# Delta-rule heads: the attention matrices move from VectorE to GpSimd, and the gate sums' fetch to an earlier wait

## What is computed

```python
gc = jnp.cumsum(g, axis=-1)
decay = jnp.exp(jnp.where(incl, gc[..., :, None] - gc[..., None, :], -jnp.inf))
lhs = eye + jnp.einsum("nbhik,nbhjk->nbhij", kb, k) * decay * (1.0 - eye)
u = solve(lhs, v * beta[..., None])
w = solve(lhs, kb * jnp.exp(gc)[..., None])
attn = jnp.einsum("nbhik,nbhjk->nbhij", q, k) * decay
...
def step(state, inp):
    v_new = u_c - jnp.einsum("bhck,bhkv->bhcv", w_c, state)
    o = jnp.einsum("bhck,bhkv->bhcv", q_c, state) + jnp.einsum("bhij,bhjv->bhiv", attn_c, v_new)
    state = state * gl[..., None, None] + jnp.einsum("bhck,bhcv->bhkv", k_c, v_new)
```

## Time and profile before

| | |
|---|---|
| median of 3 runs | 1743.07 us (1726.6 to 1747.39) |
| profiled execution | 1737.7 us |
| its span, first to last instruction | 1735.9 us |
| mean granted clock of TensorE over the span | 0.975 |
| busy: PE, DVE, ACT, POOL | 93%, 50%, 36%, 7% |

### The profile page before, as it was taken

How to read it: one execution, slowest core, us unless ns; L and a number is a source line. 1 busy time by engine, 2 the same in 40 slices (tenths; PEclk the granted TensorE clock), 3 DMA queues, 4 the chain that set the end, 5 groups by cost and what they waited for, 6 DMA issues and landing times.

```text
span 1735.9 us, 35476 instructions
## 1 busy us (share of the span) xinstructions
PE 1610.5 (93%) x14468; PEld 963.2 (55%) x14468; DVE 860.5 (50%) x1952; ACT 620.9 (36%) x1276; POOL 115.8 (7%) x278
## 2 busy tenths in 40 slices
PE   5999999999999999999999999999999888777798
PEld 2465564654755566666575766676744544333343
DVE  1372451722624567786868686868610641111163
ACT  2151531513412446464646464645400112111123
POOL 6000010000000000000000000000000022112100
PEclk9999999969999999999999999999999989999999
DMA  9230110301201212121111111111064589999741
GB/s 358 93 101 2 49 50 0 98 0 49 98 13 56 85 41 73 36 64 51 49 51 49 51 49 51 49 51 49 2 217 173 206 308 419 421 420 409 310 156 49
DMA packets 105458, 210.80 MB, mean 121 GB/s; under 512 B 10323, under 2 KB 78136, under 8 KB 92029
## 3 DMA queue, kind: packets, MB, share of 16 engines
q1 hardware_dynamic: 99256, 197.46, 31.5%
q0 software_dynamic: 4896, 8.40, 1.3%
q10 hardware_dynamic: 1188, 3.28, 0.5%
HBM read 203.73 MB, written 14.81 MB: 126 GB/s over the span
## 4 chain that ended last, share of the span: by engine, by line
PE 54%; DMA 11%; DVE 2%; ACT 2%; issue 1%; SPq 0%; DVEq 0%; POOL 0%; ACTq 0%; POOLq 0%
PE ps L1474 12%; DMA W<-in_moe_w_up_dram 10%; PE ps L1485 6%; PE ps L2497 5%; PE ps L1615 4%; PE ps L1641 4%; PE ps L3079 3%; PE ps L2893 3%; PE ps L515 2%; PE ps L1515 2%; PE ps L1495 1%; PE ps L1525 1%; PE ps L1499 1%; PE ps L1537 1%; PE ps L2906 1%; PE ps L2398 1%
## 5 line engine op out<-in xcount | busy, mean ns | idle before, releaser
L1474 PE MATMUL ps<-hT,W 128*128 128x512 f32 x512 | 231.5, 597 | 2.3 <-ACTq L95 2.2
L1474 PEld LDWEIGHTS ps<-hT,W 128*128 128x128 f32 x512 | 95.4, 191 | 99.9 <-issue 97.8
L603 PE MATMUL ps<-hT,W 128*128 128x512 f32 x288 | 145.4, 635 | 4.2 <-DVE spare L194 4.2
L1485 PE MATMUL ps<-hT,W 128*128 128x512 f32 x256 | 124.5, 615 | 0.0
L2035 DVE SCALAR_TENSOR_TENSOR arena<-ps,arena 128x510 f32<-128x510 f32 (+1 forms) x128 | 95.4, 745 | 14.1 <-ACT arena L1770 10.7
L2497 PE MATMUL ps<-W,yT 128*128 128x512 f32 x216 | 93.1, 592 | 1.3 <-DVE yT L2151 1.3
L603 PEld LDWEIGHTS ps<-hT,W 128*128 128x128 f32 x288 | 52.1, 197 | 52.8 <-issue 51.0
L1615 PEld LDWEIGHTS ps<-W,arena 64*64 64x64 f32 x2048 | 63.4, 135 | 27.9 <-issue 27.9
L2893 PE MATMUL ps<-W,yT 128*32 128x256 f32 x1024 | 58.1, 380 | 20.2 <-DMA W<-in_moe_w_gate_dram 11.8
L1615 PE MATMUL ps<-W,arena 64*64 64x32 f32 x2048 | 67.5, 220 | 6.4 <-ACT arena L1838 3.8
L2970 ACT ACTIVATE arena<-arena 128x256 f32<-128x256 f32 x48 | 20.0, 417 | 147.9 <-DVE arena L2607 136.6
(11 more groups left out here) (533 smaller groups left out, 2818.1 us busy)
## 6 DMA issues: line engine op xcount, KB each, us to landing
W<-in_w_in_dram SPq DMA_DIRECT2D x33, 512.0 KB, 6.7
W<-in_gdn_w_in_dram SPq DMA_DIRECT2D x16, 1024.0 KB, 7.0
arena<-in_moe_w_up_dram SPq DMA_DIRECT2D x16, 1024.0 KB, 6.0
arena<-in_moe_w_down_dram SPq DMA_DIRECT2D x16, 1024.0 KB, 10.0
W<-in_moe_w_up_dram SPq DMA_DIRECT2D x16, 1024.0 KB, 6.0
W<-in_moe_w_down_dram SPq DMA_DIRECT2D x16, 1024.0 KB, 5.8
W<-in_moe_w_gate_dram SPq DMA_DIRECT2D x16, 1024.0 KB, 5.7
arena<-in_moe_w_gate_dram SPq DMA_DIRECT2D x14, 1024.0 KB
```

The source lines that it names most:

```text
L603: mm = pe.matmul(ps[:, 5 + i % 2, :], w[:, k, j, :], hT[:, k, :], start=(k == 0), stop=(k == ND - 1))
L1474: mm = pe.matmul(ps[:, 6 + k0 % 2, :], wg[:, k, j * P:(j + 1) * P], hT[:, k, :], start=(k == 0), stop=(k == ND - 1))
L1485: mm = pe.matmul(ps[:, (4, 1)[e], :], wz[:, k, e * P:(e + 1) * P], hT[:, k, :], start=(k == 0), stop=(k == ND - 1))
```

## The change

`attention` goes from VectorE's list to GpSimd's, which gets a semaphore of its own in each stage (`s.pool`). GpSimd makes the matrices of chunks 0, 3, 1 and 2 in one go, behind "qk masked", "D c" and, in a turn, behind "o 3", the last reading of the old ones. TensorE's wait for "attention 2" moves from the scan's step 1 to step 0. VectorE's `masked_qk` waits for the matrices of the turn before, since it overwrites `qkm`. SyncE waits for "attention 2" of the turn before instead of this one ahead of the gate sums.

```diff
@@ sync: the loop over turns
-            sp.wait_ge(*loop.dve.at("attention 2", i))
+            sp.wait_ge(*loop.pool.at("attention 2", i - 1))
             gate_sums_in(i + 1)
             sp.wait_ge(*loop.pe.at("projected", i))
...
@@ tensor: attended(s, st)
-            if st == 1:
-                pe.wait_ge(*s.dve.at("attention 2", s.i))
+            if st == 0:
+                pe.wait_ge(*s.ago.pool.at("attention 2", s.ago.i))
...
@@ gpsimd
+        def attention(s, c):
+
+            pool.wait_ge(*s.act.at(f"D {c}", s.i))
+            for d in range(2):
+                pool.tensor_tensor(attnT[:, c, 2 * d:2 * d + 2, :], XD[:, 2 * d:2 * d + 2, c * P:c * P + P],
+                                   repeat(qkm[:, c, d, :], 2), ALU.mult).then_inc(*s.pool.step(f"attention {c}"))
+
+        s = first
+        pool.wait_ge(*s.dve.at("qk masked"))
+        for c in (0, 3, 1, 2):
+            attention(s, c)
+        s.pool.close()
+        pool.wait_ge(*s.pool.end())
+        loop.pool.credit(pool)
+        for i in range(LOOPS):
+            s = turn_of(i)
+            s.pool.begin(i)
+            pool.wait_ge(*s.pe.at(f"o {NT - 1}", s.i))
+            pool.wait_ge(*s.dve.at("qk masked", s.i))
+            for c in (0, 3, 1, 2):
+                attention(s, c)
+            s.pool.close()
...
@@ vector: masked_qk(s)
             dve.wait_ge(*s.pe.at("k q", s.i))
+            if s.ago:
+                dve.wait_ge(*s.ago.pool.at("attention 2", s.ago.i))
...
@@ vector: levels(s, scan)
             scan_columns(s, scan)
-            attention(s, 0, s)
             for lv in range(1, LEVELS):
...
-                if lv == 2:
-                    attention(s, NT - 1, s)
...
@@ vector: a turn (and the last stage in the same way)
             decayed_v(s, 0)
-            for c in (1, 2):
-                attention(s, c, s.ago)
             state(s, 0)
```

More of the change, by code:

```diff
@@ L1345, in build, with __init__ @@
     class Stage:
[L1350 to L1356, removed]
+        def __init__(self, pe, dve, act, pool, i=None, ago=None):
+            self.pe, self.dve, self.act, self.pool, self.i, self.ago = pe, dve, act, pool, i, ago
+    first = Stage(steps("first_head_products"), steps("first_head_vector"), steps("first_head_scalar"), steps("first_head_attention"))
+    loop = Stage(steps("heads_products"), steps("heads_vector"), steps("heads_scalar"), steps("heads_attention"))
+    last = Stage(steps("last_head_products"), steps("last_head_vector"), steps("last_head_scalar"), None,
+                 ago=Stage(loop.pe, loop.dve, loop.act, loop.pool, LOOPS - 1))
     def turn_of(i):
-        return Stage(loop.pe, loop.dve, loop.act, i, Stage(loop.pe, loop.dve, loop.act, i - 1))
+        return Stage(loop.pe, loop.dve, loop.act, loop.pool, i, Stage(loop.pe, loop.dve, loop.act, loop.pool, i - 1))
     def next_head(s, each):
@@ L1436, in _ @@
         gr_in.begin(LOOPS - 1)
-        sp.wait_ge(*loop.dve.at("attention 2", LOOPS - 1))
+        sp.wait_ge(*loop.pool.at("attention 2", LOOPS - 2))
         gate_sums_in(LOOPS)
@@ L2151, in gated_y @@
                 dve.tensor_tensor(yT[:, k, :], ps[:, 3 + e, :], zg[:, e, :], ALU.mult).then_inc(*s.dve.step(f"{kind}y {e}"))
[L2153 to L2159, removed]
         def changed(g, lv):
@@ L2311, in _ @@
         s.dve.close()
-    GDN = [(s, None) for s in (ab_pe, ab_dve, ab_act, ab_pool, first.pe, first.dve, first.act)]\
-        + [(s, LOOPS) for s in (loop.pe, loop.dve, loop.act)] + [(s, None) for s in (last.pe, last.dve, last.act)]
+    GDN = [(s, None) for s in (ab_pe, ab_dve, ab_act, ab_pool, first.pe, first.dve, first.act, first.pool)]\
+        + [(s, LOOPS) for s in (loop.pe, loop.dve, loop.act, loop.pool)] + [(s, None) for s in (last.pe, last.dve, last.act)]
     cut[0] = 0
```

## The result

| | before | after |
|---|---|---|
| median, us | 1743.51 (4 runs, 1726.6 to 1747.39) | 1789.63 (4 runs, 1778.83 to 1794.57) |
| profiled execution, us | 1737.7 | 1793.24 |
| its span, us | 1735.9 | 1791.5 |
| mean granted TensorE clock | 0.975 | 0.954 |

The ratio is 1.0275, 95% interval 1.0191 to 1.036: slower beyond the noise; whether by more than 2% the interval leaves open. The median lies 18.6 us above the forecast of 1771 and 0.6 us above the upper end of its range.

A forecast was written before the change was run, and what follows sets the result against it. The prediction took TensorE to bound the heads, with one VectorE piece on its path. The profiled 1737.7 us plus 21 for the hold and 12 for the clock gave 1771 us, with a range of 1740 to 1789.

The forecast's parts named there:

- What bounds the heads: Delta-rule heads, 600 to 1250 us: TensorE bounds, busy 636.76 of 650 us; one VectorE piece before level 1 on its path.
- The removal worth 0: Taking 64 multiplications, 23.1 us, off VectorE gains 0, since nobody waits for them; bounds 0 and 9 us.
- The gate sums, some 7 us sooner and worth 0: SyncE's gate-sum transfer, queued behind the z weights, goes out some 7 us sooner, not half a turn; worth 0.
- The hold on VectorE: Before level 1, GpSimd's SBUF reads block VectorE instructions with two SBUF inputs: 3.0 us a turn, 21 us over seven.
- Copies held, the count by turns: Predicated copies and GpSimd instructions alternate, one each, at 0.56 us a hold: 3.0 us a turn.
- The sign to look for, 3.2: If right, the first group's four predicated copies take some 3.2 us instead of 1.47.
- The first rival: Predicated copies before level 1 are not held: 3 us of delay, pauses of about 1.1 us, 1741 us; chance 0.16.
- the third: GpSimd starts only after the first levels, beside the convolution: price 0 to -3 us, 1736 us; chance 0.10.
- The clock: TensorE's longer pause before level 1 lowers its clock in half the turns: 3.5 x 3.4 = 12 us; bounds 0 and 24.
- the second rival: The clock falls behind the pause in every turn: 1737.7 + 21 + 24 = 1783 us, upper bound 1793; chance 0.25.
- The first head worth 0: In the first head GpSimd's eight multiplications lie beside the convolution, which reads PSUM, so the hold costs 0.
- The range: 1740 to 1789 us, taking in the first rival and most of the second, leaving out the third.

The follow-up runs named there:

- The spread order: Second z half's eighths reordered, one filling the pause before level 1: against before, 0.9959 with VectorE's multiplications; 0.9955 with them on GpSimd, started behind the second first-level transpose.
- the VectorE delay: Before, with three extra unread VectorE multiplications of 128x400 ahead of the first group's predicated copies in each turn: 1793.02 us, ratio 1.0299.
- the late gate sums: The changed kernel, with SyncE's gate-sum fetch also waiting for the first step's decayed values on VectorE: 1801.47 us, ratio 1.035.
- GpSimd late: The changed kernel, with GpSimd's multiplications in a turn also waiting for the second first-level transpose on VectorE: 1739.93 us, ratio 1.0008.
- the multiplications left out: The changed kernel with the seven turns' attention matrices made on neither engine, GpSimd only stepping its semaphore: 1770.3 us, turns 592.9 us in sum.
- GpSimd only writing: The changed kernel with sixteen GpSimd memsets of 128x256 in place of the multiplications in the turns: turns 591.4 us in sum, one run.
- the spread order of before: Before, with the second z half's eighths spread, one ahead of level 1, and VectorE's multiplications as they were: 1733.67 us, ratio 0.9959.
- the spread order with GpSimd: The changed kernel, GpSimd started behind the second first-level transpose and z's eighths spread, one ahead of level 1: 1729.19 us, ratio 0.9955.

## Why the prediction was right or wrong

**What bounds the heads: right.** TensorE, with one VectorE piece on its path. The delay put on that piece without GpSimd cost the same, and other work in the pause of before (0.75 us in the earlier trace rows, 0.62 or 0.63 in the other turns) made it go.

**The removal worth 0: right.** The spread order with and without VectorE's multiplications gives the same turns, to 0.4 us in six of them.

**The gate sums, some 7 us sooner and worth 0: right in the turns.** Holding them back by 5.5 us changed nothing there (643.8 us against 642.1); for the whole time it is not shown.

**The hold on VectorE: right in kind, 0.7 us a turn too large.** "Copies held, the count by turns" stands: GpSimd starts at the end of L1537, the two alternate, and four copies take 3.11 us. (The sign to look for, 3.2, doesn't follow from the prediction's own sum: holds of 0.5 and 1.7 on top of 1.47 are 3.7. It leaves out the hold of the first copy.) The first rival (copies not held) and the third (GpSimd too late) fall by the same rows. The term was 3.0 us a turn, 21 in all; it measured 2.3 and 16. The step that was too large is the hold of 0.56 us for each, worked out from the 512-element meetings of the earlier trace rows: the five held copies, as many as forecast, took 0.44 to 0.48 us more than the 0.461 of an undisturbed one, two of them only 0.24 and 0.26. A copy and a multiplication together took 0.73 us; with 0.56 on top of a quarter of 1.47 they would have taken 0.93.

**The clock: the step that failed.** "Half of the turns, 3.5 x 3.4 = 12 us" was 6 turns and 33.7 us. Both factors were too small. The number: I weighed the 1.90 us pause that had a fall against the 2.21 us pause that had none. The pauses of 2.46 to 2.51 us at this place brought a fall in 18 of 21 turns (this change, the VectorE delay and the late gate sums), the one of 1.25 in 1 of 7, those of 0.62 to 0.75 in none of 28 (before, GpSimd late, the multiplications left out, GpSimd only writing). And the pause at the first turn's start, the same 2.21 us, brought one here too (5.29 us for the eight L1474), as in 6 of the 11 experiments; in the other five the eight took 3.67 as before: one instance of a thing that goes either way had been taken for its rule. It goes with what lay ahead: it came in all seven executions in which the first head's level 1 has a pause of 2.41 us or more and a fall of 10.24 us behind it, and in none of the six in which these are 2.12 us or less and 6.83. The price: I took that of the first head, whose fall lasted 6.83 us, but behind the pause of a turn it lasted 13.65 and covered all of level 1 and the six L1485 behind it, 6 us instead of 3.4. Of the second rival (the clock in every turn, 1783 to 1793) the place and the sum came true, though not its factors: 16 + 34 instead of 21 to 31 + 24.

**The first head worth 0: right for the time, wrong in its reason.** "The convolution reads PSUM" is true of the convolution, but behind it L2060 (0.85 us) and L2047 (0.72 us) were held there, as their counterparts are in the turns with GpSimd late. They read one SBUF input each. The 4.3 us by which after reaches its first L1638 later are not theirs: GpSimd starts there at 617.32, when the second group's level 1 (616.15) has begun and 3.0 of the 4.3 us are already there. TensorE's pauses before the first level of that head are 0.81 and 2.74 us, and 0.62 and 2.74 in the spread order of before, which has no GpSimd there; from that level to the first L1638 the two take 30.18 and 30.21 us, each with a fall of 10.24 us. Before and the spread order with GpSimd, with shorter pauses and a fall of 6.83 us, take 28.93 and 28.92.

**The range.** It ended at 1789 because the second rival was taken in only in part; the price of a fall entered it with one value instead of bounds.

## What to carry to other kernels

Work moved to GpSimd has to be placed by what VectorE does beside it: beside work on the path of the engine that bounds, its reads put their time on that path, some microseconds away the same instructions were free. Where TensorE is the bound, a new pause can cost more than its length, so look at what TensorE runs behind it at the lower clock and price all of that; and look at several pauses of like length before taking a chance for the fall. Independent products put into the pause can be worth more than the work moved.

## What the runs showed of the hardware

- A predicated copy (mask and data in SBUF) is held beside a GpSimd instruction that reads SBUF: 461 ns alone, up to 939 beside it. The two engines then alternate, one copy and one multiplication of 128x256 in 0.73 us. Against GpSimd's memsets it is not (1.48 us for four).
- VectorE instructions with one SBUF input are held too: TENSOR_SCALAR of 128x512 takes 0.43 us alone and 0.96 beside GpSimd, that of 128x64 takes 0.19 and 0.72. The section of the Trainium skill named above says so of tensor_scalar and copies in the modes that use both ports; the rows agree in the hold, and don't show the mode.
- TensorE's clock falls with a chance, not by a rule that these rows give: the same pause with the same work behind it, 2.50 us, brought 1.2 GHz for 13.65 us in five turns, for 10.24 in one and not at all in one. What tells these turns apart is not shown.
- More work can be faster: four unused products in each turn took 35 us off the changed kernel's median, and 31.7 off its seven turns.
